# A routed expert layer on one core: GpSimd normalizes the finished rows, stores and fetches them behind the next gather, and skips padding rows

## What is computed

```python
# each token goes to 2 of 32 experts; xs holds the gathered rows in blocks
def run_block(args):
    xb, e = args
    h = jax.nn.silu(xb @ w_gate[e]) * (xb @ w_up[e])
    return h @ w_down[e]
out = zeros.at[slot_tok].add(ys * slot_gate[:, None])[:T]
...
x = x + hier_moe(n2, ...)
return rms_norm(x, final_g)
```

## Time and profile before

| | us |
|---|---|
| median of 3 runs | 2107.91 |
| lowest, highest | 2102.77, 2109.08 |
| the profiled execution | 2109.44 |
| its span, first to last instruction | 2107.5 |
| PE busy in it | 1989.9 |
| DVE, ACT, POOL busy | 1323.2, 1157.9, 833.3 |
| mean granted clock of PE, share of full | 0.978 |

### The profile page before, as it was taken

One profiled execution on the slowest core, in us unless ns is written; L12 is line 12 of the kernel. 1 busy time (PEld: TensorE's weight loads), 2 busy tenths in 40 slices (PEclk: granted clock), 3 DMA queues, 4 the chain that ended last, 5 costly groups with the idle time before them and its releaser, 6 DMA issues. The chain is left out here.

```text
span 2107.5 us, 39825 instructions
## 1 busy us (share of the span) xinstructions
PE 1989.9 (94%) x12627; PEld 1696.8 (81%) x12628; DVE 1323.2 (63%) x2411; ACT 1157.9 (55%) x2421; POOL 833.3 (40%) x1024
## 2 busy tenths in 40 slices
PE   7999999979999999989999688999999999999997
PEld 5888888857777787868778577888888888888886
DVE  5333333338888888845565568777776667795763
ACT  4211111128888889853333267666666657674662
POOL 2322222213656644431332344444444434443443
PEclk9999999989999999999999899999999999999999
DMA  7433333365363543224544579988889988997863
GB/s 224 148 117 120 118 120 121 112 182 151 106 171 99 132 107 91 69 70 161 183 137 150 199 269 367 327 283 299 301 287 313 327 266 295 345 373 241 303 209 87
DMA packets 230708, 420.62 MB, mean 200 GB/s; under 512 B 27290, under 2 KB 165146, under 8 KB 206529
## 3 DMA queue, kind: packets, MB, share of 16 engines
q1 hardware_dynamic: 201312, 351.34, 48.8%
q0 software_dynamic: 29296, 68.03, 12.7%
HBM read 344.35 MB, written 110.41 MB: 216 GB/s over the span
## 5 line engine op out<-in xcount | busy, mean ns | idle before, releaser
L742 ACT ACTIVATE prob<-score,nmax 128x512 f32<-128x512 f32 (+3 forms) x464 | 263.8, 578 | 25.8 <-DVE nmax L892 25.4
L60 PE MATMUL proj<-w_in_lo,n1T_hi 128*128 128x512 f32 (+1 forms) x640 | 243.9, 381 | 3.4 <-DVE w_in_lo L245 3.3
L62 PE MATMUL proj<-w_in_hi,n1T_hi 128*128 128x512 f32 (+1 forms) x640 | 238.8, 373 | 0.0
L892 DVE TENSOR_REDUCE nmax<-score 128x2 f32<-128x1024 f32 (+3 forms) x232 | 212.5, 920 | 41.8 <-PE score L940 40.3
L61 PE MATMUL proj<-w_in_hi,n1T_lo 128*128 128x512 f32 (+1 forms) x640 | 238.7, 373 | 0.0
L60 PE MATMUL u_ps<-wu_lo,xT_hi 128*128 128x256 f32 x752 | 216.9, 288 | 0.0
L61 PE MATMUL u_ps<-wu_hi,xT_lo 128*128 128x256 f32 x752 | 213.4, 284 | 0.0
L62 PE MATMUL u_ps<-wu_hi,xT_hi 128*128 128x256 f32 x752 | 213.4, 284 | 0.0
L1879 DVE TENSOR_TENSOR wg_lo<-raw_pieces,wg_hi 128x1024 fp32r<-128x1024 f32 x124 | 148.0, 1221 | 92.3 <-ACT wg_hi L1840 92.3
L807 POOL TENSOR_SCALAR prob<-prob,scale,lam 128x512 f32<-128x512 f32 (+3 forms) x168 | 136.8, 826 | 154.4 <-DVE scale L879 144.8
L264 DVE TENSOR_TENSOR cosx<-proj,rope_sb 128x512 f32<-128x512 f32 (+1 forms) x64 | 37.8, 591 | 213.3 <-PE proj L62 209.5
(11 more groups left out here) (261 smaller groups left out, 5176.8 us busy)
## 6 DMA issues: line engine op xcount, KB each, us to landing
raw_pieces<-in_w_down SPq DMA_DIRECT2D x64, 1024.0 KB, 10.6
raw_pieces<-in_w_gate SPq DMA_DIRECT2D x62, 1024.0 KB, 8.2
raw_pieces<-in_w_up SPq DMA_DIRECT2D x62, 1024.0 KB, 7.7
qk_scratch<-qkT SPq DMA_DIRECT2D x94, 256.0 KB, 2.6
xT_sb<-in_xT SPq DMA_DIRECT2D x16, 512.0 KB, 5.0
h<-in_x SPq DMA_DIRECT2D x16, 512.0 KB, 6.5
acc_scratch<-h SPq DMA_DIRECT2D x16, 512.0 KB, 3.1
n_scratch<-n SPq DMA_DIRECT2D x16, 512.0 KB, 5.6
```

What stands on the lines that cost most here:

```text
L60: pe.matmul(out, hi, w_lo, start=first, stop=False)
L62: return pe.matmul(out, hi, w_hi, start=False, stop=last)
L742: act.activation(prob[:, n % RING, c, 0:w], score[:, n % BUFS, c, 0:w], ACT.Exp, bias=nmax[:, c, n:n + 1], accum_out=part[:, c, n:n + 1]). ...
L892: dve.tensor_reduce(nmax[:, :, n:n + 1], score[:, n % BUFS, :, 0:w], AX.X, ALU.max, negate=True).then_inc(max_ready, 1)
```

## The change

Four things are done in the stage `experts`.

1. `normalize(b)` leaves DVE's `one_block` and goes to POOL, as two instructions (scale by the root, then multiply by the gain) instead of one.
2. The store and the fetch of finished rows, which stood behind `scale` and at the end of POOL's iteration, now stand right behind the gather of the next block and ahead of the addition. What is fetched in iteration b is thus what iteration b - 1 made ready.
3. ACT squares the finished rows behind Silu instead of ahead of it.
4. The gather and the addition get a bounds check: rows of index 2048 and more (padding) are skipped. `x` is cleared once at the start.

```diff
                 def fetch_whole(b):
-                    pool.wait_ge(at_ready, b * 2 + 6)
-                    pool.wait_ge(final_ready, b + 2)
+                    pool.wait_ge(at_ready, b * 2 + 4)
+                    pool.wait_ge(final_ready, b + 1)
...
+                def normalize(b):
+                    pool.wait_ge(rstd_ready, b + 2)
+                    pool.wait_ge(stored, b * 16 + 16)
+                    pool.sem_inc(passed, 1)
+                    pool.tensor_scalar(whole[:, :], whole[:, :], rstd[:, :], None, ALU.mult).then_inc(whole_scaled, 1)
+                    pool.wait_ge(whole_scaled, b + 1)
+                    pool.tensor_tensor(final[:, :], whole[:, :], g_bc[:, :], ALU.mult).then_inc(final_ready, 1)
...
                     gather(b + 1, within(after))
+                    store(b, b * 2 + 4)
+                    fetch_whole(b)
                     add(b)
-                    scale(b)
-                    store(b)
+                    normal_root(b)
+                    normalize(b)
+                    aim_store(b)
                     move_on(b)
                     pool.tensor_copy(own[:, :].bitcast(I32), slots[:, bass.ds(within(here), 1), :].bitcast(I32))\
                         .then_inc(own_ready, 1)
-                    fetch_whole(b)
...
                 blocks = block_count(pool)
+                store(blocks, blocks * 2 + 4)
+                fetch_whole(blocks)
...
-                    highs(0)
-                    square(b)
-                    highs(1, 2)
+                    highs(0, 1, 2)
                     act.wait_ge(g_done, b + 1)
                     act.wait_ge(h_turned, b * 2 + 1)
                     act.activation(hid[:, :], g_ps[:, :], ACT.Silu).then_inc(silu_ready, 1)
+                    square(b)
                     highs(3, 4, 5)
                     copy_hT(b, 0)
...
                     lows(0, 1, 2)
-                    normalize(b)
                     dve.wait_ge(silu_ready, b + 1)
                     hidden(b, 0)
```

More of the change, by code:

```diff
@@ L1657, in experts @@
         last_in = sem("p6_last_in")
+        x_cleared = sem("p6_x_cleared")
+        whole_scaled = sem("p6_whole_scaled")
         last_step = sem("p6_last_step")
@@ L1722, in gather @@
                     pool.indirect_dma_start(x[:, :], None, n2_d,
-                                            bass.IndirectOffsetOnAxis(ap=fetch[:, :], axis=0)).then_inc(x_in, 16)
+                                            bass.IndirectOffsetOnAxis(ap=fetch[:, :], axis=0),
+                                            bounds_check=SEQ - 1, oob_is_err=False).then_inc(x_in, 16)
                 def add(b):
@@ L1729, in add @@
                     pool.indirect_dma_start(acc_d, bass.IndirectOffsetOnAxis(ap=own[:, 0:1].bitcast(I32), axis=0),
-                                            y[:, :], None, compute_op=ALU.add).then_inc(own_free, 16)
+                                            y[:, :], None, bounds_check=SEQ - 1, oob_is_err=False,
+                                            compute_op=ALU.add).then_inc(own_free, 16)
                 def fetch_whole(b):
-                    pool.wait_ge(at_ready, b * 2 + 6)
-                    pool.wait_ge(final_ready, b + 2)
+                    pool.wait_ge(at_ready, b * 2 + 4)
+                    pool.wait_ge(final_ready, b + 1)
                     pool.sem_inc(passed, 1)
@@ L1738, in fetch_whole, with normal_root @@
                                             bounds_check=SEQ - 1, oob_is_err=False).then_inc(whole_in, 16)
-                def scale(b):
+                def normal_root(b):
                     pool.wait_ge(ss_ready, b + 1)
@@ L1746, in scale, with aim_store @@
                     pool.tensor_tensor(rstd[:, :], var[:, :], power[:, 0:1], ALU.pow).then_inc(rstd_ready, 1)
-                def store(b):
+                def aim_store(b):
                     pool.wait_ge(stored, b * 16 + 16)
@@ L1751, in store @@
                     pool.tensor_copy(final_at[:, :], whole_at[:, :]).then_inc(at_ready, 1)
-                    pool.wait_ge(at_ready, b * 2 + 5)
-                    pool.wait_ge(final_ready, b + 2)
+                def store(b, aimed):
+                    pool.wait_ge(at_ready, aimed)
+                    pool.wait_ge(final_ready, b + 1)
                     pool.sem_inc(passed, 1)
@@ L1783, in _ @@
                 pool.memset(y[:, :], 0.0).then_inc(y_ready, 1)
+                pool.memset(x[:, :], 0.0).then_inc(x_cleared, 1)
+                pool.wait_ge(x_cleared, 1)
                 pool.wait_ge(own_free, 32)
@@ L1789, in _ @@
                 pool.tensor_copy(final_at[:, :], own[:, 2:3].bitcast(I32)).then_inc(at_ready, 1)
-                pool.wait_ge(at_ready, 4)
-                pool.indirect_dma_start(whole[:, :], None, acc_d, bass.IndirectOffsetOnAxis(ap=whole_at[:, :], axis=0),
-                                        bounds_check=SEQ - 1, oob_is_err=False).then_inc(whole_in, 16)
-                pool.indirect_dma_start(out, bass.IndirectOffsetOnAxis(ap=final_at[:, :], axis=0), final[:, :], None,
-                                        bounds_check=SEQ - 1, oob_is_err=False).then_inc(stored, 16)
+                pool.wait_ge(g_in, 16)
                 pool.sem_inc(own_ready, 1)
@@ L1803, in _ @@
                                         bass.IndirectOffsetOnAxis(ap=own[:, 0:1].bitcast(I32), axis=0)).then_inc(last_in, 16)
-                scale(blocks)
+                normal_root(blocks)
+                aim_store(blocks)
                 pool.wait_ge(last_step, 2)
@@ L1808, in _ @@
                 pool.tensor_tensor(last_stat[:, 2:3], last_stat[:, 1:2], power[:, 0:1], ALU.pow).then_inc(last_step, 1)
-                store(blocks)
+                store(blocks + 1, blocks * 2 + 5)
                 pool.wait_ge(last_step, 5)
```

## The result

The changed kernel takes **2375.7 us** (median of 4 runs, 2367.6 to 2377.5), the kernel before 2108.5 (4 runs beside it): ratio 1.1265, 95% interval 1.1231 to 1.1299. It is slower by 267 us where the forecast said slower by 10. The profiled execution has a span of 2374.2 us against 2107.5. Executions that took far longer than the others of the same kernel are left out of all times here.

A forecast was written before the change was run, and what follows sets the result against it. PE was taken to bound the stage, with some 20 us to win. 2109.4 - 19.7 + 28.9 + 1.5 = 2120.1, less 1.5 to the runs' median: 2119 us. Range 2093 to 2143, the forecast's own 2113 to 2135, chance 0.42.

The forecast's parts named there:

- the size of the loop: POOL's loop from one square to the next, 20.2 us summed, against the 18.0 us of an undisturbed block.
- the step that let only 16 of the 46 turns exceed their block: PE waits only in one-block experts: 7 behind a pair at 1.3 us, 9 followers at 2.2, together 28.9 us.
- Rival C: The port bounds: replaced blocks take DVE POOL's 3.3 us of reads besides its 17; 2138 to 2154 us, chance 0.10.
- Rivals A and B: A: POOL's loop at 18.0, no new waits, 2090 us, chance 0.27. B: loop 19.2 to 19.7, 2103 to 2110, 0.21.
- scale and multiply: POOL's two operations in its loop: scale 1.4 us, multiply 1.9, and 1.2 for DVE's low part in between.
- copies and issues: In POOL's loop: three small copies and gaps 1.0 us; from `own` to the fetch's issue 5.0 us.
- the landing: Fetch of `whole` in POOL's loop: 7.6 us to land while weights stream, from a range of 7.6 to 8.5.
- a pair costs nothing: Where SP pauses the landing is 2.4 to 4, so a pair's loops, 20.2 + 14 or so, stay under 36 us.
- the 19.7 us of gain: Square behind Silu and normalize off DVE remove all 11 PE waits for `hid` and the clock loss.
- Own and addition: The addition, issued some 2.5 us later, still releases `own` 2 us before ACT's `y` needs it; costed at 0.
- Rival D: `own` comes too late: addition at M + 11, landing 12.6, just in time at M + 24.4; given no time of its own.
- The end: After the last block, store and fetch stand ahead of the last read of `x`, which lands later: 1.5 us more.

## Why the prediction was right or wrong

**Right: the direction, the mechanism and its place.** GpSimd's loop is longer than a block, the square waits for the DMA of `whole`, and PE waits in front of `y_ps` for `hT_lo`. The waits for `hid` are gone but for 1.1 us. The direction was held with a chance of 0.51 only. What failed is the size of the loop, 20.2 us in the sum and 24.2 in the mean (27.1 in replaced blocks), and the step that let only 16 of the 46 turns exceed their block; 267 us were measured where these two steps gave 10. Rival C is out: VectorE's subtractions take 1.24, 1.29 and 1.22 us in the mean (about 1.22 before), so it is GpSimd that gives way and not VectorE, other than in the one meeting of the earlier trace rows. Rivals A and B would have needed a turn of 18 to 19.7.

**Wrong by itself: scale and multiply, 4.5 in my sum, 7.25 measured.** The scale was priced with 1.4 us from the slope of L807 and takes 2.85. The multiply was given 1.9 from L337 and takes 2.38. The collision was 1.2 and is 0.9 to 1.0 for each of the two where it happens.

**Wrong: copies and issues, 1.0 and 5.0 in my sum, 2.4 and 6.8 measured.** I let VectorE meet GpSimd's arithmetic only. It meets everything: in the turn above the copy of `own` takes 1.07 us and the store's issue 1.84, where the run with short subtractions has 0.19 and 1.04 in the mean. The turn in the earlier trace rows already had a copy of 0.64 and an addition of 2.56 that could have told this. The Trainium skill ("SBUF — State Buffer", Who interferes with whom) has the rule that I weighed and applied to one operation of a turn: a VectorE instruction with two SBUF inputs contends with a GpSimd instruction that reads SBUF, and issue order decides who blocks. The run with short subtractions agrees, 2.8 us a turn.

**Wrong: the landing, 7.6 in my sum, 10.3 measured where two experts of one block follow each other.** I took the shorter end because of the padding. The fetch was the first of its row in the kernel before (issued right behind `own`) and is the third now, in a stretch in which the weights stream; only the price of the old place was in the earlier trace rows. The runs showed that both count: 4.3 us without the stream, 5.9 with the fetch first.

**Wrong: "a pair costs nothing".** That needed 20.2 + 14 under 36. It is 27.1 + 18.2 = 45.3, so every turn binds. 31 turns exceed my 20.2 by 6.9 us in the mean and the 15 others my 14 by 4.2: 277 us. At the forecast's prices the loops sum to 31 x 20.2 + 15 x 14 = 836 us, its blocks to 828 + 28.9 + 1.8 = 859; this room of 23 is used up first, and 254 are left, which is what the stretch between first and last mark has over the forecast's (1112.5 - 858.7). Had only the forecast's 16 turns counted, it would have been 16 x 6.9 = 110 of the 254. (The terms of the loop as recorded add up to 20.15 and not 20.25, which changes nothing.)

**Wrong: the 19.7 us of gain.** The waits for `hid` go, but in the kernel before they could not be had by moving square and normalization alone (2131 instead of 2106). In the changed kernel the term is drowned. The clock, expected at 1.00 from 1300 on, is 0.91, where the kernel before has 1.00 from 1300 to 2080; PE pauses in nearly every block now (window: busy us of PE, PEld, DVE, ACT, POOL, then clock, DMA share, GB/s):

```profile
1300.00:2340.00 1040.00, 840.86 (x4658) 730.39 (x4657) 514.59 (x553) 514.13 (x637) 656.02 (x518) 0.91 0.65 210
```

I take this to cost little, since the square waits for the fetch and not for PE in 45 of 48 cases, so that slower matmuls only shorten PE's waits; no run tested it.

**Own and addition, forecast at 0.** Rival D happened as well: ACT waited 49.8 us, in 16 cases, for `own` in front of `y`. What that cost isn't shown.

**The end, forecast at 1.5.** From the last mark to the end of the span it is 28.65 us against 22.07, so 6.6. The last read of `x` and the addition behind it, to be held against the earlier trace rows:

```profile
2355.03 0.97 POOL L1818 DMA_INDIRECT x<-acc_scratch,own  x1 [0.30 <-issue]
```

```profile
2360.37 1.23 DVE L1947 TENSOR_TENSOR x<-x,y 128x1024 f32<-128x1024 f32 x1 [10.19 <-DMA x<-acc_scratch,own]
```

The read is issued 9.5 us after the last mark. In the kernel before it was 1.9. I had counted from an undelayed block.

**The range.** Its upper end, 2143, was set in the lower half of rival C. The longest loop that was priced, 22 us, took the landing and the two operations at their upper values but left "16 blocks only" as it was (57.7 us). The uncertain terms were all parts of one loop that was already 2.2 us longer than a block, and once every turn binds, each microsecond counts 46 times.

## What to carry to other kernels

When work goes onto an engine whose queue also issues the transfers, sum that engine's whole loop, and price every instruction in it (copies and issues too) at its contended value if VectorE streams two-input operations beside it. Then multiply the excess by all turns before deciding that some turns have room. A transfer's landing depended here on its place among the others of its queue and on the stream beside it, so it can't be taken from its old place; and a store that must land before its buffer is reused should not stand behind an accumulating transfer.

## What the runs showed of the hardware

- `tensor_scalar` on GpSimd with one scalar by partition took 2.85 us for 128x1024 fp32, more than a multiply of two tensors of that size (2.38), and 1.55 for 128x512, while L807 took 0.925 for 128x512. Why these differ is open.
- Beside VectorE's subtractions, one after another, these operations of GpSimd were two-valued: 2.85 or 3.75, 2.38 or 3.39, 0.19 or 1.07, and for a DMA issue 1.04 or 1.84 us. VectorE's own means stayed within 0.07 us of those before.
- The same indirect fetch (up to 128 rows of 4 KB, 44 in the mean) landed in 3.7 us without the weights' stream and in 9.8 with it (DMA share 0.33 and 0.78 in that stretch). Issued ahead of the gather, it landed in 3.5 us beside the full stream (share 0.77).
- The store, issued behind an accumulating transfer, landed 11.9 us after its issue, ahead of it 8.4; the accumulating transfer itself took 11.3 to 11.4 in both.
- With shorter subtractions on VectorE the fetch landed later (11.1 instead of 9.8 us). I have no explanation that a run supports.
